# Head distances of a Mamba-2 mixer built as rounded high and low tiles on ScalarE instead of as one float32 tile on GpSimd

## The reference, cut to what matters

```
acs = cumsum(dt * a_neg)                      # per head, within a chunk of 128 tokens
decay = exp(acs[t] - acs[s])  for s <= t, else 0
y_intra = (C_t . B_s) * decay[t, s] @ (x_s * dt_s)
w_end = exp(acs[last] - acs);  y_inter = C_t . state * exp(acs[t])
```

## Time and profile before

| | |
|---|---|
| median of 3 runs | 1619.88 us (1619.72 to 1620.32) |
| profiled execution | 1620.02 us, of which span 1618.3 us |
| PE busy | 1580.8 us, 98% of the span |
| DVE busy | 1047.0 us, 65% |
| ACT busy | 731.1 us, 45% |
| POOL busy | 215.0 us, 13% |
| granted TensorE clock | 0.994 of full speed |

### The profile page before, as it was taken

One profiled execution on the slowest core, in us unless ns is written; L12 is line 12 of the kernel. 1 busy time (PEld: TensorE's weight loads), 2 busy tenths in 40 slices (PEclk: granted clock), 3 DMA queues, 4 the chain that ended last, 5 costly groups with the idle time before them and its releaser, 6 DMA issues.

```text
span 1618.3 us, 24373 instructions
## 1 busy us (share of the span) xinstructions
PE 1580.8 (98%) x9778; PEld 1383.6 (86%) x9778; DVE 1047.0 (65%) x1287; ACT 731.1 (45%) x885; POOL 215.0 (13%) x182
## 2 busy tenths in 40 slices
PE   7999989999999999999999999899999999999997
PEld 6888788999999978888888888888999999788886
DVE  5554489788876555454665455888888765554545
ACT  6344343445445345443564445344344533544444
POOL 1000023353330000000000000243344100000000
PEclk9999999999999999999999999999999999999999
DMA  8555534465445645555565555345544465466551
GB/s 257 193 182 183 180 106 132 129 181 140 146 130 182 207 157 194 202 181 183 174 191 184 187 185 147 111 128 154 174 138 130 155 200 187 142 210 196 190 182 65
DMA packets 245077, 270.92 MB, mean 167 GB/s; under 512 B 12560, under 2 KB 226152, under 8 KB 245012
## 3 DMA queue, kind: packets, MB, share of 16 engines
q1 hardware_dynamic: 239504, 266.90, 52.2%
q10 hardware_dynamic: 5364, 2.98, 0.7%
q0 software_dynamic: 144, 0.15, 0.0%
HBM read 268.94 MB, written 1.05 MB: 167 GB/s over the span
## 4 chain that ended last, share of the span: by engine, by line
PE 86%; DVE 8%; issue 3%; ACT 2%; POOL 1%; DMA 1%; SPq 0%; POOLq 0%; ACTq 0%; DVEq 0%
PE bank L1377 27%; PE bank L1403 16%; PE bank L1405 16%; PE bank L1404 16%; DVE xcv L1048 2%; DVE w_lo L823 2%; PE bank L1447 1%; PE bank L1563 1%; PE bank L1766 1%; PE bank L1625 1%; PE bank L1569 1%; DVE xcv L1045 1%; PE bank L1398 1%; DMA w_raw<-in_w_ffn_dram 1%; DVE bcv L1048 1%
## 5 line engine op out<-in xcount | busy, mean ns | idle before, releaser
L823 DVE TENSOR_TENSOR w_lo<-w_raw,w_hi 128x2048 fp32r<-128x2048 f32 x248 | 580.6, 2344 | 287.2 <-ACT w_hi L518 287.2
L518 ACT ACTIVATE w_hi<-w_raw 128x2048 fp32r<-128x2048 f32 x248 | 473.2, 1912 | 214.6 <-PE bank L1405 114.3
L1377 PE MATMUL bank<-u_hi,w_hi 128*128 128x256 f32 x1152 | 335.9, 292 | 2.6 <-DVE u_lo L866 2.6
L1377 PE MATMUL bank<-u_lo,w_hi 128*128 128x256 f32 x1152 | 322.1, 280 | 0.0
L1377 PE MATMUL bank<-u_hi,w_lo 128*128 128x256 f32 x1152 | 321.9, 279 | 0.0
L1403 PE MATMUL bank<-w_hi,ha_hi 128*128 128x512 f32 x704 | 279.4, 397 | 1.8 <-DVE ha_lo L866 0.9
L1405 PE MATMUL bank<-w_hi,ha_lo 128*128 128x512 f32 x704 | 275.4, 391 | 0.0
L1404 PE MATMUL bank<-w_lo,ha_hi 128*128 128x512 f32 x704 | 274.9, 390 | 0.0
L1377 PEld LDWEIGHTS bank<-u_hi,w_hi 128*128 128x128 f32 x1152 | 219.1, 190 | 9.5 <-issue 8.7
L1377 PEld LDWEIGHTS bank<-u_lo,w_hi 128*128 128x128 f32 x1152 | 219.0, 190 | 5.1 <-issue 4.8
L1377 PEld LDWEIGHTS bank<-u_hi,w_lo 128*128 128x128 f32 x1152 | 219.0, 190 | 0.0
(11 more groups left out here) (274 smaller groups left out, 2368.3 us busy)
## 6 DMA issues: line engine op xcount, KB each, us to landing
w_raw<-in_w_ffn_dram SPq DMA_DIRECT2D x262, 512.0 KB, 4.2
w_raw<-in_w_in_dram SPq DMA_DIRECT2D x160, 512.0 KB, 4.9
w_raw<-in_w_branch_b_dram SPq DMA_DIRECT2D x32, 512.0 KB, 4.5
w_raw<-in_w_branch_a_dram SPq DMA_DIRECT2D x16, 512.0 KB, 4.5
w_raw<-in_w_out_dram SPq DMA_DIRECT2D x16, 512.0 KB, 3.9
w_raw<-in_w_ple_gate_dram SPq DMA_DIRECT2D x16, 512.0 KB, 4.6
y_feat<-in_w_ple_dram ACTq DMA_DIRECT2D x2, 1024.0 KB, 4.9
h<-in_x_dram SPq DMA_DIRECT2D x2, 512.0 KB, 5.7
```

The costliest lines, as they stand in the source:

```text
L518: a_.activation(whi[slot][:, :, :], raw[slot][:, :, :], ACT.Copy).then_inc(sem["w_hi"], 1)
L823: v_.tensor_tensor(wlo[slot][:, :, :], raw[slot][:, :, :], whi[slot][:, :, :].bitcast(F32), ALU.subtract).then_inc(sem["w_lo"], 1)
L1377: i = mm(o, w[slot][:, k, cs], x[:, k, :], start=(k + q == 0 and not seeded), stop=(k == KD - 1 and q == 2 and not seeded), skip_group_che ...
```

## The change

R becomes two `fp32r` tiles, `R_hi` and `R_lo`, from `dA_hi` (dA rounded) and `dA_lo` (dA less dA_hi), which VectorE makes once a layer. ScalarE builds them, with one 128x128 ACTIVATE (Copy with a per-partition scale) for each head and part: 8 for a half, 32 for a group. GpSimd builds none. Each matmul on R becomes two `fp32r` matmuls, with `fp32r` copies of `tri_gt` and `ones` that are made once. The buffers move: R_hi lies over `xwe` and `zth`, R_lo over `xw`; some other tiles are placed anew.

```
-            def distances_of(g, c, half):
-                g_.tensor_tensor(R[half][:, :, :], tri_le[:, :].unsqueeze(1).broadcast_to([P, 4, P]),
-                                 dA[:, c, bass.ds(g * EH + 4 * half, 4)].unsqueeze(2).broadcast_to([P, 4, P]),
-                                 ALU.mult).then_inc(sem["r_built"], 1)
...
+                    def part_of(dst, part, g, c, half):
+                        for e in range(4):
+                            i = a_.activation(dst[half][:, e, :], tri_le[:, :], ACT.Copy,
+                                              scale=part[:, c, bass.ds(g * EH + (4 * half + e), 1)].bitcast(F32))
+                        return i
+                    def distances_of(g, c, half):
+                        part_of(R_hi, dA_hi, g, c, half)
+                        part_of(R_lo, dA_lo, g, c, half).then_inc(sem["r_built"], 1)
...
+                    def decay(c, b):
+                        act.wait_ge(sem["seg_done"], G * 6 + (2 * c + b + 1))
...
+                                      ACT.Exp).then_inc(sem["exp_done"], 1)
+                        if c == 0:
+                            distances_of(g, 1, b)
...
+                        act.wait_ge(sem["dA_split"], lay + 1)
+                        distances_of(g, 0, 0)
+                        distances_of(g, 0, 1)
...
                     else:
-                        decay(0)
+                        decay(0, 0)
+                        tanh_conv(0, bcv[:, :, :])
+                        decay(0, 1)
+                        step(2)
                         step(3)
+                        decay(1, 0)
+                        decay(1, 1)
                         tanh_conv(1, xcv[:, 0:2, :])
                         score_exp()
-                        decay(1)
...
+                    if not last:
+                        act.wait_ge(sem["yi_done"], G + 1)
+                        act.wait_ge(sem["zth_ready"], G * 2 + 2)
+                        for half in range(2):
+                            part_of(R_hi, dA_hi, g + 1, 0, half)
                     act.wait_ge(sem["ha32_ready"], G + 1)
...
+                    if not last:
+                        act.wait_ge(sem["y_done"], G + 1)
+                        for half in range(2):
+                            part_of(R_lo, dA_lo, g + 1, 0, half).then_inc(sem["r_built"], 1)
                     scaled(GA)
...
-                        mm(bank[4 + 2 * c + half][:, :], tri_gt[:, :], R[half][:, :, :], start=True, stop=True)\
+                        mm(bank[4 + 2 * c + half][:, :], tri_gt_r[:, :], R_hi[half][:, :, :], start=True, stop=False)
+                        mm(bank[4 + 2 * c + half][:, :], tri_gt_r[:, :], R_lo[half][:, :, :], start=False, stop=True)\
                             .then_inc(sem["seg_done"], 1)
```

More of the change, by code:

```diff
@@ L111, in trunk @@
         g_fin = gate_a[:, 0:4, :].rearrange("p a b -> p (a b)")
+        top[0] = place(top[0], 64)
+        tri_gt_r = sb("tri_gt_r", [P, P], F32R)
+        ones_r = sb("ones_r", [P, P], F32R)
         ident = sb("ident", [P, P])
@@ L164, in trunk @@
         cth, a = at("cth", [P, 2, S], F32, a)
+        a = place(a, 64)
         late = a
+        xwe_at = late + NC * EH * HP * 4
         xw, a = at("xw", [P, NC, EH * HP], F32, a)
@@ L175, in trunk @@
         xin, a = at("xin", [P, 2, 2, S + 3], F32, a)
+        a = place(a, 64)
+        zth_at = a
         zth, a = at("zth", [P, 2, S], F32, a)
-        R = (xwe[:, :].rearrange("p (e t) -> p e t", e=4),
-             zth[:, :, :].rearrange("p a b -> p (a b)").rearrange("p (e t) -> p e t", e=4))
+        R_hi = [at(f"R_hi{b}", [P, 4, P], F32R, off)[0] for b, off in enumerate((xwe_at, zth_at))]
+        R_lo = [at(f"R_lo{b}", [P, 4, P], F32R, late + b * 4 * P * 4)[0] for b in range(2)]
         vtok, a = at("vtok", [P, NC, 258], F32, a)
@@ L206, in trunk @@
         row_one, a4 = at("row_one", [1, DEPTH, 104], F32, a4)
-        a5 = late
+        a5 = xcv_at
         r_i, a5 = at("r_i", [MH, S], F32, a5)
@@ L212, in trunk @@
         r_w, a5 = at("r_w", [MH, S], F32, a5)
+        assert a5 == xcv_at + 4 * S * 4
+        a5 = late + 4 * S * 4
         pre_row, a5 = at("pre_row", [40, S], F32, a5)
@@ L420, in row_norm, with group @@
                 power(n + 1, "var_ready", var[:, :], "rms_ready", rms[:, :])
-            def distances_of(g, c, half):
-                g_.tensor_tensor(R[half][:, :, :], tri_le[:, :].unsqueeze(1).broadcast_to([P, 4, P]),
-                                 dA[:, c, bass.ds(g * EH + 4 * half, 4)].unsqueeze(2).broadcast_to([P, 4, P]),
-                                 ALU.mult).then_inc(sem["r_built"], 1)
-            def group(lay, g, first, last):
+            def group(lay, g):
                 G = pool.snap(lay * NG + g)
@@ L443, in token_columns @@
                     g_.tensor_copy(gtk[:, :].unsqueeze(2), tokc[:, :, bass.ds(g, 1)]).then_inc(sem["gtk_ready"], 1)
[L445 to L455, removed]
+                token_columns()
                 pool.wait_ge(sem["p_exp"], G + 1)
@@ L470, in group @@
                 power(G + 1, "hvar_ready", hvar[:, :], "hrms_ready", hrms[:, :])
[L471 to L475, removed]
                 pool.wait_ge(sem["ysq_ready"], G + 1)
@@ L483, in _ @@
                 g_.memset(M4[:, :, :], 0.0).then_inc(sem["m4_clear"], 1)
[L484 to L487, removed]
+                with nc.gpsimd.Fori(0, NG) as g:
+                    group(lay, g)
                 power(lay + 1, "yvar_ready", var[:, :], "yrms_ready", rms[:, :])
@@ L719, in body @@
                                   scale=0.5).then_inc(sem["gate_tanh"], 1)
[L721 to L723 removed]
+                body(0, True, False)
+                with nc.scalar.Fori(1, NG - 1) as g:
+                    body(g, False, False)
+                body(NG - 1, False, True)
             for lay in range(DEPTH):
@@ L984, in softplus_gates @@
                                         op0=ALU.mult, op1=ALU.mult).then_inc(sem["dA_ready"], 1)
+                dve.wait_ge(sem["dA_ready"], lay + 1)
+                ch.add(v_.tensor_copy(dA_hi[:, :, :], dA[:, :, :]))
+                ch.wait()
+                v_.tensor_tensor(dA_lo[:, :, :], dA[:, :, :], dA_hi[:, :, :].bitcast(F32), ALU.subtract)\
+                    .then_inc(sem["dA_split"], 1)
             def gate_rows(lay):
@@ L1228, in _ @@
             dve.wait_ge(sem["const_ready"], 2)
+            ch.add(v_.tensor_copy(tri_gt_r[:, :], tri_gt[:, :]))
+            ch.add(v_.tensor_copy(ones_r[:, :], ones[:, :]))
             dve.wait_ge(sem["in_loaded0"], 16)
@@ L1568, in from_start @@
                             pe.wait_ge(sem["exp_done"], G * 4 + (3 + half))
-                            mm(bank[6 + half][:, :], ones[:, :], R[half][:, :, :], start=True, stop=True)\
+                            mm(bank[6 + half][:, :], ones_r[:, :], R_hi[half][:, :, :], start=True, stop=False)
+                            mm(bank[6 + half][:, :], ones_r[:, :], R_lo[half][:, :, :], start=False, stop=True)\
                                 .then_inc(sem["seg_done"], 1)
```

26 lines of the change are left out of this document (13 added, 13 removed).

## The result

The changed kernel takes 1633.82 us (median of 4 runs, 1630.92 to 1635.01); the kernel before took 1620.10 beside it (4 runs). The ratio is 1.0081 with a 95% interval of 1.0065 to 1.0097: slower by 0.8%. The profiled execution is the shortest of the four, 1630.92 us with a span of 1629.2, so the traces are 10.9 us apart, where the medians are 13.7 apart.

What follows compares the result with a forecast made beforehand. TensorE bounds a loop group, with a ScalarE-VectorE ring less than 3 us beneath; -0.1, 2 x 2.25 and +2.9, less 1.0, give +6.3 a layer, +12.6 in all: 1632.6 profiled, 1632.5 median, range 1614 to 1642.

Steps and rivals of the forecast that it cites:

- the first, the ring: Likeliest case: ScalarE and VectorE's chain of mutual waits lengthens each loop group; 1632.5 us, range 1628 to 1638, chance 0.5.
- TensorE's saving: Matmuls on R: two fp32r ones 0.23 us apart replace one float32 of 0.86; 0.40 saved each, 19 us in all.
- The copies: ScalarE's builds of R: 0.31 us each, 2.5 for eight, 10 for a group's 32.
- the two cases that hung on 0.17 and on 0.42: ScalarE's builds: 0.17 down to 0.10 us each, 1602 to 1616, chance 0.16; 0.42 without overlap, 1645, chance 0.13.
- The 0.29: ScalarE's build of one 128-column copy, estimated from 280 ns, 0.833 ns a column and 93 ns overlap: 0.29 us.
- The ring: ScalarE-VectorE chain from one `ha32_ready` to the next: +1.1 at first tanh, +4.1 at V's lo tile, +2.9 at `hn`, +2.25 finally.
- GpSimd behind `mask_cb`: GpSimd's three multiplies there hold up VectorE: 2.4 us lost before, up to 2.3 more now, of which 1.5 taken.
- The estimate by the Trainium skill: Behind `mask_cb`, the shared port pair held for whole instructions makes VectorE lose the whole 2.3 us, 3.7 at `hn`.
- The waits of TensorE: TensorE waits 2.6 us at segments (1,1), about 2 ahead of `hn`'s transposes; 19 us less work, 32 us more waits.
- Group 0: Each layer's first group: +0.5 us at the end, -0.6 for the last lo tile, so -0.1.
- The loop groups: Groups after the first: 2.25 us more for each of two, 2.9 at the last `hn` less 1.0, per layer.
- By layer: Each layer's mixer: -0.1, 2 x 2.25 and +2.9, less 1.0, giving +6.3 us; +12.6 for two.

Runs made afterwards that it cites:

- the two doses of eight copies: Changed kernel plus eight more ScalarE copies that nobody reads: directly ahead of the lo copies, behind the square of y, 1645.45 us; directly behind the hi copies 1632.32 us.
- the matmuls alone: Kernel before in the changed kernel's placement, each fp32 matmul on R made two rounded ones reading one GpSimd-built tile twice: 1618.50 us.
- the placement's time: Kernel before with only its SBUF tiles placed at the changed kernel's addresses, no new instruction: 1619.26 us.
- the copies alone: Changed kernel with ScalarE's hi and lo builds kept, but one fp32 matmul per half, on the hi tile: 1629.11 us.

## Why the prediction was right

Predicted 1632.5, measured 1633.82; the case was the first, the ring.

- *TensorE's saving.* The rounded matmuls start 0.23 apart (239.35, 239.58, 239.81, 240.04), as taken, and none of it shows in a loop group: with ScalarE's copies in place, fp32 matmuls give the same 66.09.
- *The copies.* Eight take 2.43 to 2.44 us, 0.31 each: as taken. This closes the two cases that hung on 0.17 and on 0.42. The 0.29 that the prediction worked out from the Trainium skill's figures (ScalarE: Activation LUTs; they stand in the section What ACT_TABLE_LOAD costs, not in the one that the prediction names) is 4% short of 2.44 / 8 = 0.305.
- *The ring.* Lengths from the start of the square of y: the first tanh came 0.66 us later (predicted 1.1), VectorE's lo tile of V 3.5 later (4.1), `hn` 2.7 later (2.9), and the whole loop group grew by 2.06 (2.25). That this place is in the ring, and the one ahead of `ha_hi` isn't, the two doses of eight copies show (2.33 and 0.00).
- *GpSimd behind `mask_cb`.* I took 1.5 us more than the 2.4 lost before; it is 4.3 less 2.4, 1.9. The estimate by the Trainium skill (SBUF — State Buffer, SBUF: two separate sides), by which the port pair is held for the whole instruction, was 2.3; the 1.9 lies midway between it and my 1.5. The 2.85 us that fall to 0.69 agree with its rule.
- *The waits of TensorE.* At segments (1,1) 2.04 us, predicted 2.6; at `hn` 0.7 to 1.5, predicted about 2. At `cst` in group 0 they grew from 0.94 to 2.24. The sum was too high on both sides: TensorE's busy time fell by 15.1 us, not 19, and its idle time grew by 26.0, not 32. Part of the first is the granted clock, at half of which a matmul is busy for longer.
- *Group 0* was off by the largest amount: -0.1 predicted, its heads came 1.65 us later in layer 1 and 0.3 in layer 2. The term itself was near. Of the 1.65, 1.45 lie between `cst` and the heads (12.35 us, 10.90 before), where the changed kernel had its 3.4 us at half the granted clock; the prediction has no term for that. Layer 2's 0.3 compares unlike clocks: up to its heads the kernel before had 10.2 us at half the clock in that layer, the changed one 6.8.
- *The loop groups,* the ring's own part: 12.8 predicted for both layers together (2.25, 2.25 and 2.9 less 1.0 in each), 11.2 measured.
- *By layer* 6.3 was predicted, 7.1 and 6.1 measured.
- *Not foreseen:* 3.3 us less in the merge loops, by the placement; 3.0 us more behind `cst` in the two groups 0, by the granted clock; 1.1 us more at the start. The profiled execution is 1.7 us under the 1632.6 predicted for it, the median 1.3 over the 1632.5. The mechanism was right; that the number is this close is partly the luck that these terms nearly cancel.

The runs of the two parts say it shortest: the matmuls alone took 0.8 us off the placement's time, the copies alone added 9.1 to the time before, and both together added 13.7.

## What to carry to other kernels

Before giving a busy engine's work to an idle one, follow the chain of waits through the idle one: an engine that is busy 28 of 64 us can still set the length of the loop, and the place of an instruction in its queue decides whether its length is paid. Test a place with a dose: a few more instructions of the same kind, at the suspected place and at one with a wait behind it. In this case the same copies, put into the two waits (ahead of `ha_hi`, and ahead of the first tanh) turned 0.8% slower into 0.5% faster.

## What the runs showed that I had not expected

- A wait of 2.04 us on TensorE was followed by 3.4 us at half the granted clock, in which 256-column matmuls started 0.21 us apart instead of 0.12. It isn't so each time. In the loop groups of all profiled executions 22 waits of 2.0 to 3.5 us stand at the matmuls on R, and within 1.5 us of the end of 11 of them (three of the changed kernel's six) the clock fell; at 21 waits of 0.5 to 1.8 us it never did. So a cheaper matmul can lengthen a wait and cost clock.
- The merge loop's iterations follow the placement of tiles, 16.87 or 17.29 us; moving its own tiles alone isn't what does it.
- GpSimd's broadcast of the parameter row at the start took 0.50 us in most profiled executions and 2.1 to 2.4 in others, among them the changed kernel's. It doesn't by itself tell when the mixer begins: the wait for dA ended at 230.56 in the kernel before and at 231.66 in the changed one, but at 232.07 with ScalarE's part alone, where the broadcast took 0.50.
